# Attention in two layers: exponentials placed ahead of copies on ScalarE, and the rounding of output weights placed behind a head's step

## The chip, the cores and the metric

The kernel runs on one core of a Trainium2 chip. The metric is the device time of the whole program in microseconds. Five engines run side by side, each through an instruction list of its own in fixed order, and they wait for one another on semaphores: TensorE (PE, with PEld for its weight loads), VectorE (DVE), ScalarE (ACT), GpSimd (POOL) and SyncE (SP), whose queue loads the weights.

## The reference

Two transformer layers (an even and an odd one), then a block with a delta rule. Only the two attention mixers matter here. Each projects 256 tokens, runs 16 heads of width 64 over them, and multiplies the 16 heads' results by an output weight of 1024 x 1024:

```python
def even_mixer(xn, w_in, w_out, ...):
    qa, ka, va, qi, ki, wi, qb, kb, vb = _split(xn @ w_in, EVEN_SPLITS)
    ...
    ya = dsa_sparse_attention(qa, ka, va, qi, ki, wi)      # kind A: keys picked by top_k
    yb = chunked_relpos_attention(qb, kb, vb, rel_bias)    # kind B
    return jnp.concatenate([ya, yb], axis=-1) @ w_out

def odd_mixer(xn, w_in, w_out, forget_b, sinks, rope_h):
    qc, kc, vc, fc, qd, kd, vd = _split(xn @ w_in, ODD_SPLITS)
    ...
    yc = forgetting_attention(qc, kc, vc, log_f)           # kind C
    yd = sink_window_gqa(qd, kd, vd, sinks)                # kind D
    return jnp.concatenate([yc, yd], axis=-1) @ w_out

# every kind:  p = softmax(q @ k.T * scale + bias or mask);  y = p @ v
```

Everything is float32. A product with weights is done as three products of rounded halves: high x high, high x low, low x high.

## The kernel before

**Weights.** All weights come as a stream of slots of 128 x 2048 numbers. For each slot SP loads `raw` (ring of 3), ACT writes the rounded half `whi` (`split`, L1839, 128x2048), and the remainder `wlo = raw - whi` follows: on DVE (L2370, 128x2048), or, for the *shared* slots, its second half on DVE (L2366, 128x1024) and its first half on POOL (L1022, 128x1024). The slots of the last two output groups and the first slots of the next stage are shared ones. PE multiplies with L1182 to L1184. A slot is split two slots ahead of its use (AHEAD = 2), and its `raw` buffer is loaded anew when both remainders are written.

**Positions.** A mixer is a list of positions `at` that each engine walks through in the same order. First come the projection parts, four to a block (`("proj", block, i)`; even 28 positions, odd 20), then 16 output parts, four to a group g (`("out", g, sub)`), each 6 products of 512 columns. At each position an engine does its share of the part and then calls `attend(layer, step)`, with step = at - 15 (even) or at - 11 (odd).

**Heads.** Heads go in pairs. Head e has step e in the odd layer; in the even layer heads 0 to 7 have steps 0 to 7 and heads 8 to 15 steps 12 to 19. So a pair's *first head* (even e) has an odd `at` and its *second head* (odd e) an even `at`. At the first head's step PE makes the logits of both (L1355). Then, for a head of step s:

- DVE at step s: logits plus bias and their minimum, from PSUM (L2635); the second head's directly behind the first's if its step comes next
- ACT at step s: two exponentials with their sums (L1992; kind D also one of the sinks, L1990)
- scaling by 1/sum: for heads 0 to 7 on POOL (L1032, L1035), for heads 8 to 15 on DVE at step s+1 (L2641, L2644, two instructions of 128x128 and 128x256)
- PE at step s+2: three transposes into bank 6 (L1323); they wait for the scaling and for ACT's copy of the head before, since there is one bank
- ACT at step s+2: copy of bank 6 to `probT` (L1978)
- behind a pair's second head, at the position three behind its step: PE sums the values of the pair (L1336), ACT rounds them (`mhi`, L1982), DVE writes the remainder (`mlo`, L2649)

**ACT's order at a position before the change:** copy of a block (L1936), `split` of a slot, copy of turned tiles (L1944), then attend: `probT` of head s-2, `mhi`, exponentials of head s. In a projection part the split stands at i = 0 and 2, in the output at the first part of each group. **DVE's order:** `split` (in the output at the second part of each group), then attend: minimum of head s, scaling of head s-1, `mlo`. Three output splits have an effect: those at the first parts of groups 0, 1 and 2.

The lines of PE that show the transposes' two waits:

```python
pe.wait_ge(*S["probs_copied"].at((layer, e - 1)))
pe.wait_ge(*S["probs_scaled" if e < POOL_HEADS else "probs_divided"].at((layer, e)))
for j in range(3):
    last = nc.tensor.transpose(ps[:, 6, j * P:(j + 1) * P], prob[:, e % 3, j * P:(j + 1) * P], ident)
```

Of the kernel before, what the change touches and what calls it, by code (L numbers as in the profile page):

```python
# [46 lines left out]
AHEAD = RING - 1  # L47
# [77 lines left out]
OUT_SLOT = (2, 3, 0, 1)  # L125
# [350 lines left out]
def out_order(layer, g):  # L476

    return (0, 1, 2, 3) if g else FIRST_PARTS[layer]
# [4 lines left out]
FIRST_STEP = {"even": 4 * 3 + 3, "odd": 4 * 2 + 3}  # L483
# [13 lines left out]
def step_at(layer, s):  # L497

    return STEPS[layer][s] if 0 <= s < len(STEPS[layer]) else NOTHING


def head_at(layer, s):

    what, e = step_at(layer, s)
    return e if what == "head" else None
# [19 lines left out]
def mixed_tile(p):  # L525

    return 2 * OUT_SLOT[p // 2] + p % 2
# [93 lines left out]
def build(nc, dram, counted, stop=None):  # L621
# [3 lines left out]
    slot_of = {}  # L625
# [3 lines left out]
    with ctx:  # L629
# [1199 lines left out]
        def _(act):  # L1829
            split_to = [0]  # L1830

            def split(last):

                while split_to[0] <= min(last, len(plan) - 1):
                    n = split_to[0]
                    act.wait_ge(weights_loaded[n % RAW], 16 * (n // RAW + 1))
                    if n >= RING:
                        act.wait_ge(*S["weights_used"].at(n - RING))
                    act.activation(used(whi, n), used(raw, n), ACT.Copy).then_inc(*S["weights_high"].one((n, 1)))  # L1839
                    split_to[0] += 1  # L1840
# [130 lines left out]
            def attend(layer, s):  # L1971

                e = head_at(layer, s - 2)
                if e is not None:
                    act.wait_ge(*S["probs_turned"].at((layer, e)))
                    if e >= 4:
                        act.wait_ge(*S["values_done"].at((layer, (e - 4) // 2)))
                    act.activation(probT[:, e % 4, :], ps[:, 6, 0:3 * P], ACT.Copy).then_inc(*S["probs_copied"].one((layer, e)))  # L1978
                p = pair_at(layer, s - 3)
                if p is not None:  # L1980
                    act.wait_ge(*S["values_done"].at((layer, p)))
                    act.activation(mhi[:, mixed_tile(p), :], ps[:, 7, p % 2 * TOK:(p % 2 + 1) * TOK], ACT.Copy)\  # L1982
                        .then_inc(*S["mixed_high"].one((layer, p)))
                e = head_at(layer, s)
                if e is not None:
                    kind, h = head_of(layer, e)
                    for t in range(TT):
                        act.wait_ge(*S["logits"].at((layer, e, t)))
                        if t == TT - 1 and kind == "D":
                            act.activation(sunk[:, e % 4, :], lowest[:, e % 4, :], ACT.Exp, bias=row_at["sinks"][:, h:h + 1])  # L1990
                        at = prob[:, e % 3, tile_logits(t)]
                        last = act.activation(at, at, ACT.Exp, bias=lowest[:, e % 4, t:t + 1], scale=-1.0,  # L1992
                                              accum_out=total[:, e % 4, t:t + 1])
                    last.then_inc(*S["exps"].one((layer, e)))
# [252 lines left out]
            first_norm()  # L2247
            for li, (layer, blocks) in enumerate(LAYERS):
                for at, place in enumerate(POSITIONS[layer]):
                    if at == 4 * len(blocks) and blocks[-1][0] not in ROTATED:  # L2250
                        copy_block(layer, blocks, len(blocks) - 1, 1)
                    if place:
                        what, a, i = place
                        if what == "proj":
                            if i % 2 == 0:
                                split(slot_of[((layer, blocks[a][0]), i // 2)] + AHEAD)
                            if i == 3 and blocks[a][0] not in ROTATED:
                                copy_block(layer, blocks, a, 0)
                            if i == 0 and a and blocks[a - 1][0] not in ROTATED:
                                copy_block(layer, blocks, a - 1, 1)  # L2260
                        elif i == out_order(layer, a)[0]:
                            split(slot_of[(f"{layer}_out", OUT_SLOT[a])] + AHEAD - (a == 3))
                    if place in TURNS[layer]:
                        copy_turned(layer, blocks, *TURNS[layer][place])
                    if layer == "even" and place in INDEX_AT:
                        index_relus(INDEX_AT[place])
                    if layer == "odd" and place == ("proj", 1, 1):
                        gate_logs()
                    if layer == "odd" and place == FORGET_SPLIT_AT:
                        forget_high()  # L2270
                    attend(layer, at - FIRST_STEP[layer])
                norm_behind_out(2 * li + 1, slot_of[(f"{layer}_out", OUT_SLOT[3])])
                up(li)
                norm_behind_down(2 * li + 2, slot_of[(f"down{li}", FT // 2 - 1)])
# [75 lines left out]
        def _(dve):  # L2350
# [69 lines left out]
            def norm_behind_out(k, last):  # L2420

                add_to_x(k, last, 0, (0, 1), 0)
                split(last + 2)
                normalize(k, [0])
                add_to_x(k, last, 1, (0,), 0)
                lows(k, [(0, 0), (0, 1)])
                add_to_x(k, last, 1, (1,), 0)
                normalize(k, [1])
                lows(k, [(1, 0), (1, 1)])
# [537 lines left out]
            for li, (layer, blocks) in enumerate(LAYERS):  # L2967
                for at, place in enumerate(POSITIONS[layer]):
                    if layer == "even" and place == ("proj", 0, 3):
                        dve.wait_ge(consts_loaded, 16)  # L2970
                        dve.wait_ge(rows_loaded, 16)
                        dve.wait_ge(ident_loaded, 16)
                        dve.tensor_tensor(pick_row[:, 0:8], ident[:, 0:8], ident[:, 32:40], ALU.add)\
                            .then_inc(*S["rows_low"].one("pick"))
                    if place:
                        what, a, i = place
                        if what == "proj":
                            if i == 3 and blocks[a][0] in ROTATED:
                                rope_block(layer, blocks, a, 0)
                            if i == 0 and a and blocks[a - 1][0] in ROTATED:  # L2980
                                rope_block(layer, blocks, a - 1, 1)
                            if i % 2:
                                split(slot_of[((layer, blocks[a][0]), i // 2)] + AHEAD)
                        elif i == out_order(layer, a)[1]:
                            split(slot_of[(f"{layer}_out", OUT_SLOT[a])] + AHEAD - (a == 3))
                    if layer == "even":
                        if place == ("proj", 1, 2):
                            for t in range(TT):
                                index_keys(t)
                        if place == ("proj", 2, 2):  # L2990
                            dve.wait_ge(*S["bias_ready"].at(1))
                            link(dve.tensor_scalar(bias[:, :, :], bias[:, :, :], 8.0, None, ALU.mult))
                        if place in INDEX_AT:
                            index_sums(INDEX_AT[place])
                        if place in TOP_AT:
                            take_top(TOP_AT[place])
                        if place == ("proj", 6, 1):
                            pick()
                    else:
                        if place == ("proj", 1, 0):  # L3000
                            gate_inputs()
                        if place == ("proj", 1, 2):
                            gate_finish()
                            dve.wait_ge(*S["gate_made"].at("sinks"))
                        if place == FORGET_SPLIT_AT:
                            forget_low()
                        if place in FORGET_AT:
                            forget_biases(FORGET_AT[place])
                    attend(layer, at - FIRST_STEP[layer])
                norm_behind_out(2 * li + 1, slot_of[(f"{layer}_out", OUT_SLOT[3])])  # L3010
                up(li)
                norm_behind_down(2 * li + 2, slot_of[(f"down{li}", FT // 2 - 1)])
# [131 lines left out]
```

## Time and profile before

| | |
|---|---|
| median of 3 runs | 1208.64 us (1208.52 to 1208.86) |
| the profiled execution | 1204.78 us, of which the span of the trace is 1203.0 us |
| busy: PE, DVE, ACT, POOL | 97%, 70%, 58%, 27% of the span |
| mean granted clock of TensorE | 0.997 |
| loads of weights | 1024 KB each, 4.8 us from issue to landing |
| even mixer, output parts | from 102.5 to 135.9 us of the span |
| odd mixer, heads and output parts | from 350.9 to 418.5 us of the span |

The timeline of one engine, cut to a few microseconds, gives each instruction's start and duration; in square brackets stands how long the engine was idle before it, and what ended that. Rows of different engines are put side by side by their start times. The table's last two rows are the two stretches to which the change belongs.

### The profile page before, as it was taken

The numbers are of one execution on the slowest core, as the hardware profiler recorded it, in microseconds if no ns is written. First come the engines' busy times: TensorE is split into PE (matmuls) and PEld (weight loads), VectorE is DVE, ScalarE is ACT, GpSimd is POOL, SyncE is SP. The second block draws the span as 40 slices with busy tenths as digits, with TensorE's granted clock in tenths as the row PEclk, the third lists the DMA queues.
The fourth block names the chain that finished last, engine by engine and source line by source line (L and its number), as shares of the span: only waits on it lengthen the run. The fifth ranks groups of instructions, "written<-read, shape, count | busy, mean of one in ns | idle before, by whom it ended". The sixth has DMA issues, their size and how long they took to land.

```text
span 1203.0 us, 21393 instructions
## 1 busy us (share of the span) xinstructions
PE 1170.6 (97%) x8616; PEld 1087.1 (90%) x8616; DVE 841.6 (70%) x1519; ACT 701.7 (58%) x1181; POOL 320.0 (27%) x257
## 2 busy tenths in 40 slices
PE   8999999999999999999999999999999999999997
PEld 7777899998877799998889999998989989999886
DVE  6796588884675579885568787888954565555456
ACT  5475576663458566664366667766667445444344
POOL 1172200000016300000166666575555320000000
PEclk9999999999999999999999999999999999999999
DMA  7633355556553356555343332332222646555542
GB/s 285 252 140 140 123 211 206 184 181 219 175 191 125 129 208 219 196 208 210 128 160 126 121 115 105 133 114 98 94 83 106 227 170 224 210 183 203 202 155 81
DMA packets 31587, 199.74 MB, mean 166 GB/s; under 512 B 4289, under 2 KB 6481, under 8 KB 8706
## 3 DMA queue, kind: packets, MB, share of 16 engines
q1 hardware_dynamic: 29506, 189.27, 43.6%
q0 software_dynamic: 1840, 8.60, 1.9%
q8 instruction: 68, 1.11, 0.4%
q10 hardware_dynamic: 144, 0.52, 0.1%
q14 instruction: 29, 0.24, 0.1%
HBM read 197.33 MB, written 1.05 MB: 165 GB/s over the span
## 4 chain that ended last, share of the span: by engine, by line
PE 83%; DVE 8%; ACT 4%; issue 2%; POOL 1%; DMA 0%; SPq 0%; POOLq 0%; DVEq 0%; ACTq 0%
PE ps L1182 24%; PE ps L1183 23%; PE ps L1184 23%; PE ps L1559 1%; PE ps L1575 1%; DVE ps L2824 1%; DVE wlo L2370 1%; PE ps L1336 1%; DVE conv L2755 1%; PE ps L1355 1%; PE ps L1323 1%; PE ps L1189 1%; PE ps L1207 1%; DVE halves L2472 1%; PE ps L1276 1%
## 5 line engine op out<-in xcount | busy, mean ns | idle before, releaser
L1182 PE MATMUL ps<-halves,whi 128*128 128x256 f32 x1472 | 409.8, 278 | 0.2
L1184 PE MATMUL ps<-halves,wlo 128*128 128x256 f32 x1472 | 404.8, 275 | 0.0
L1183 PE MATMUL ps<-halves,whi 128*128 128x256 f32 x1472 | 404.8, 275 | 0.0
L2370 DVE TENSOR_TENSOR wlo<-raw,whi 128x2048 fp32r<-128x2048 f32 (+1 forms) x133 | 301.3, 2268 | 112.2 <-ACT whi L1839 108.7
L1839 ACT ACTIVATE whi<-raw 128x2048 fp32r<-128x2048 f32 (+1 forms) x143 | 269.5, 1887 | 102.4 <-PE ps L1184 96.3
L1182 PEld LDWEIGHTS ps<-halves,whi 128*128 128x128 f32 x1472 | 282.5, 192 | 0.8 <-DVE halves L2963 0.5
L1184 PEld LDWEIGHTS ps<-halves,wlo 128*128 128x128 f32 x1472 | 282.6, 192 | 0.0
L1183 PEld LDWEIGHTS ps<-halves,whi 128*128 128x128 f32 x1472 | 282.5, 192 | 0.1
L1106 POOL TENSOR_TENSOR wlo<-raw,whi 128x1024 fp32r<-128x1024 f32 x72 | 172.5, 2404 | 51.0 <-ACT whi L1848 50.4
L1000 POOL TENSOR_TENSOR rstd<-sumsq,half_power 128x1 f32<-128x1 f32 x14 | 11.3, 809 | 573.3 <-ACT xn L1866 406.0
L1182 PE MATMUL ps<-whi,halves 128*128 128x512 f32 (+4 forms) x440 | 148.2, 337 | 4.8 <-DVE halves L2472 4.0
L1184 PE MATMUL ps<-whi,halves 128*128 128x512 f32 (+4 forms) x440 | 143.8, 327 | 0.0
L1183 PE MATMUL ps<-wlo,halves 128*128 128x512 f32 (+4 forms) x440 | 143.7, 327 | 0.0
L1182 PE MATMUL ps<-whi,hhi 128*128 128x512 f32 x264 | 100.2, 379 | 0.5 <-DVE hf L2689 0.5
L1183 PE MATMUL ps<-wlo,hhi 128*128 128x512 f32 x264 | 100.1, 379 | 0.0
L1184 PE MATMUL ps<-whi,hlo 128*128 128x512 f32 x264 | 100.1, 379 | 0.0
L1182 PEld LDWEIGHTS ps<-whi,halves 128*128 128x128 f32 x440 | 83.6, 190 | 16.0 <-issue 8.5
L2824 DVE SCALAR_TENSOR_TENSOR ps<-glu_in,par,ps 128x256 f32<-128x256 f32 x224 | 94.5, 480 | 0.0
L1184 PEld LDWEIGHTS ps<-whi,halves 128*128 128x128 f32 x440 | 83.8, 190 | 5.8
L1183 PEld LDWEIGHTS ps<-wlo,halves 128*128 128x128 f32 x440 | 83.7, 190 | 4.9
L2017 ACT ACTIVATE cv<-ps,par 128x256 f32<-128x256 f32 x88 | 44.9, 561 | 73.3 <-PE ps L1184 67.2
L1848 ACT ACTIVATE whi<-raw 128x1024 fp32r<-128x1024 f32 x72 | 76.5, 1064 | 7.8 <-PE ps L1184 7.8
(337 smaller groups left out, 1849.5 us busy)
## 6 DMA issues: line engine op xcount, KB each, us to landing
raw<-in_stream SPq DMA_DIRECT2D x176, 1024.0 KB, 4.8
gain<-in_gains POOLq DMA_DIRECT2D x7, 512.0 KB, 5.7
bias<-in_rel POOLq DMA_DIRECT2D x1, 1536.0 KB, 8.6
raw<-in_stream SPq DMA_DIRECT2D x2, 648.0 KB, 7.3
cst<-in_consts POOLq DMA_DIRECT2D x1, 1280.5 KB, 5.9
raw<-in_stream SPq DMA_DIRECT2D x2, 528.0 KB, 4.2
x<-in_x SPq DMA_DIRECT2D x2, 512.0 KB, 4.3
out<-xn SPq DMA_DIRECT2D x4, 256.0 KB, 2.5
```

Source lines behind the costliest of these rows:

```text
L1106: pool.tensor_tensor(wlo[:, n % RING, c], raw[:, n % RAW, c], whi[:, n % RING, c].bitcast(F32), ALU.subtract).then_inc(*S["pool_weights_lo ...
L1182: nc.tensor.matmul(out, a_hi, b_hi, start=start, stop=False)
L1183: nc.tensor.matmul(out, a_hi, b_lo, start=False, stop=False)
L1184: return nc.tensor.matmul(out, a_lo, b_hi, start=False, stop=stop)
L1189: nc.tensor.matmul(ps[:, bank, 0:P], ident, ident, start=True, stop=True)
L1207: last = nc.tensor.transpose(to_evens_first(out) if k in TOKENS_EVENS_FIRST else out, xn[:, t, (4 * half + i) * P:(4 * half + i + 1) * P], ...
L1276: last = nc.tensor.transpose(ps[:, 3, i * P:(i + 1) * P], temp[:, b % 2, t, i * P:(i + 1) * P], ident)
L1839: act.activation(used(whi, n), used(raw, n), ACT.Copy).then_inc(*S["weights_high"].one((n, 1)))
L1848: act.activation(whi[:, n % RING, c], raw[:, n % RAW, c], ACT.Copy).then_inc(*S["weights_high"].one((n, half)))
L2017: act.activation(cv[:, j % 2, m, :], ps[:, up_bank(j), m * TOK:(m + 1) * TOK], ACT.Identity, bias=par_at(f"conv_b{li}", c), scale=par_at(f ...
L2370: dve.tensor_tensor(used(wlo, n), used(raw, n), used(whi, n).bitcast(F32), ALU.subtract)\
L2824: dve.scalar_tensor_tensor(odd_taps[:, :] if k == 29 else sums, src, w, sums, ALU.mult, ALU.add)\
```

## The change

No instruction is added or taken away; three things are moved.

- ACT, at even positions of the odd layer (from the projection on) and of the even layer's output parts: the exponentials of step s, which are those of a second head, come first at the position, ahead of the block copy, the split, the turned copy, `probT` and `mhi`. At odd positions they stay where they were.
- ACT: the splits of the output groups come behind attend and the exponentials of their position.
- DVE: the splits of the output groups come behind attend of their position.

```diff
@@ scalar: attend is cut in two
                     act.activation(mhi[:, mixed_tile(p), :], ...)
+
+            def exponentials(layer, s):
+
                 e = head_at(layer, s)
@@ scalar: the positions
                 for at, place in enumerate(POSITIONS[layer]):
+                    step = at - FIRST_STEP[layer]
+                    exps_ahead = at % 2 == 0 and (at >= 4 * len(blocks) or layer == "odd")
+                    if exps_ahead:
+                        exponentials(layer, step)
                     if at == 4 * len(blocks) and blocks[-1][0] not in ROTATED:
                         copy_block(layer, blocks, len(blocks) - 1, 1)
...
-                        elif i == out_order(layer, a)[0]:
-                            split(slot_of[(f"{layer}_out", OUT_SLOT[a])] + AHEAD - (a == 3))
...
-                    attend(layer, at - FIRST_STEP[layer])
+                    attend(layer, step)
+                    if not exps_ahead:
+                        exponentials(layer, step)
+                    if place and place[0] == "out" and place[2] == out_order(layer, place[1])[0]:
+                        split(slot_of[(f"{layer}_out", OUT_SLOT[place[1]])] + AHEAD - (place[1] == 3))
@@ vector: the positions
-                        elif i == out_order(layer, a)[1]:
-                            split(slot_of[(f"{layer}_out", OUT_SLOT[a])] + AHEAD - (a == 3))
...
                     attend(layer, at - FIRST_STEP[layer])
+                    if place and place[0] == "out" and place[2] == out_order(layer, place[1])[1]:
+                        split(slot_of[(f"{layer}_out", OUT_SLOT[place[1]])] + AHEAD - (place[1] == 3))
```

## Rows read from the trace of the kernel before

**Rows 1.** The page, part 1: busy us (share of the span) xinstructions.

```profile
PE 1170.6 (97%) x8616; PEld 1087.1 (90%) x8616; DVE 841.6 (70%) x1519; ACT 701.7 (58%) x1181; POOL 320.0 (27%) x257
```

**Rows 2.** PE's waits, whole span: waiter <- awaited: us, times, longest us.

```profile
PE ps L1323 <- DVE prob L2644: 2.1, 1, 2.1
...
PE ps L1323 <- ACT probT L1978: 1.5, 3, 0.9
```

**Rows 3.** Timeline of PE, even output parts: start, duration, what [idle before].

```profile
105.63 0.93 PE L1355 MATMUL ps<-fm 64*128 64x128 f32 x8
...
110.18 0.52 PE L1323 MATMUL ps<-ident,prob 128*128 128x128 f32 x3 [2.13 <-DVE prob L2644]
...
111.83 0.49 PE L1323 MATMUL ps<-ident,prob 128*128 128x128 f32 x3
...
113.05 0.93 PE L1355 MATMUL ps<-fm 64*128 64x128 f32 x8
...
117.56 0.55 PE L1323 MATMUL ps<-ident,prob 128*128 128x128 f32 x3 [0.28 <-ACT probT L1978]
...
121.24 0.52 PE L1323 MATMUL ps<-ident,prob 128*128 128x128 f32 x3
...
122.90 0.49 PE L1323 MATMUL ps<-ident,prob 128*128 128x128 f32 x3
```

**Rows 4.** Timeline of ACT, the same stretch.

```profile
104.33 1.90 ACT L1839 ACTIVATE whi<-raw 128x2048 fp32r<-128x2048 f32 x1
...
110.73 0.49 ACT L1978 ACTIVATE probT<-ps 128x384 f32<-128x384 f32 x1 [2.03 <-PE ps L1323]
...
114.34 0.40 ACT L1992 ACTIVATE prob<-prob,lowest 128x128 f32<-128x128 f32 x1 [0.79 <-DVE lowest L2635]
...
115.23 1.90 ACT L1839 ACTIVATE whi<-raw 128x2048 fp32r<-128x2048 f32 x1
117.03 0.47 ACT L1978 ACTIVATE probT<-ps 128x384 f32<-128x384 f32 x1
```

**Rows 5.** Timeline of DVE, the same stretch.

```profile
106.25 1.23 DVE L2366 TENSOR_TENSOR wlo<-raw,whi 128x1024 fp32r<-128x1024 f32 x1 [1.53 <-ACT whi L1839]
107.39 0.28 DVE L2635 CUSTOM_DVE_ANT_0 prob<-ps,picked 128x128 f32<-128x128 f32 x1
...
108.14 1.89 DVE L2644 TENSOR_SCALAR prob<-prob,inverse 128x128 f32<-128x128 f32 x2
109.95 0.28 DVE L2635 CUSTOM_DVE_ANT_0 prob<-ps,picked 128x128 f32<-128x128 f32 x1
...
114.01 0.29 DVE L2635 CUSTOM_DVE_ANT_0 prob<-ps,picked 128x128 f32<-128x128 f32 x1 [2.76 <-PE ps L1355]
...
115.23 0.41 DVE L2649 TENSOR_TENSOR mlo<-ps,mhi 128x256 fp32r<-128x256 f32 x1
115.57 0.28 DVE L2635 CUSTOM_DVE_ANT_0 prob<-ps,picked 128x128 f32<-128x128 f32 x1
```

**Rows 6.** Timeline of POOL, the same stretch.

```profile
106.30 3.39 POOL L1022 TENSOR_TENSOR wlo<-raw,whi 128x1024 fp32r<-128x1024 f32 x1 [15.25 <-ACT whi L1839]
...
132.98 2.38 POOL L1022 TENSOR_TENSOR wlo<-raw,whi 128x1024 fp32r<-128x1024 f32 x1 [3.07 <-ACT whi L1839]
```

**Rows 7.** Timeline of PE, odd layer.

```profile
359.26 0.52 PE L1323 MATMUL ps<-ident,prob 128*128 128x128 f32 x3 [1.63 <-POOL prob L1035]
...
389.08 0.55 PE L1323 MATMUL ps<-ident,prob 128*128 128x128 f32 x3 [0.94 <-ACT probT L1978]
...
394.42 0.49 PE L1323 MATMUL ps<-ident,prob 128*128 128x128 f32 x3
```

**Rows 8.** Timeline of DVE, odd layer, first heads.

```profile
356.04 2.29 DVE L2370 TENSOR_TENSOR wlo<-raw,whi 128x2048 fp32r<-128x2048 f32 x1 [1.98 <-ACT whi L1839]
```

**Rows 9.** Timeline of POOL, the same stretch.

```profile
356.38 2.74 POOL L1035 TENSOR_SCALAR prob<-prob,inverse 128x256 f32<-128x256 f32 x1
```

**Rows 10.** Timeline of ACT, odd layer, split at the first output part.

```profile
386.76 1.90 ACT L1839 ACTIVATE whi<-raw 128x2048 fp32r<-128x2048 f32 x1
```

## The prediction, made before the result was known

> **What bounds the kernel now.** First the page's busy shares: PE is busy for 97% of the span [rows 1]. So nothing that the other engines do counts unless PE waits for it, and all that a new order can give is PE's idle time. Then PE's list of waits, for the transposes of the scaled exponentials (L1323) alone: one wait of 2.1 us for DVE's scaling, three of 1.5 us together for ACT's `probT` [rows 2]; in PE's timeline of the odd layer one of 1.63 us for POOL's scaling [rows 7]. Together some 5 us, 0.4% of the time: the ceiling of the gain. Then the timelines of PE, ACT, DVE and POOL beside one another, in the output parts, to see what stood in front of what. There ACT's rounding (1.90 us) stands before `probT` at 117.03, and PE's transpose follows it at 117.56 [rows 3, 4]: the wait that the change aims at. The wait at 110.18 is another matter. DVE's two scaling instructions started at 108.14 and took 1.89 us [rows 5]; POOL's half of a split ran from 106.30 to 109.69, and the scaling ended 0.34 us behind it, at 110.03 [rows 5, 6].
>
> **Rules that I read from the rows.** (a) POOL's half takes 2.38 us undisturbed and 3.39 us when DVE's half (1.23 us) began 0.05 us before it [rows 5, 6]; so these two exclude each other, and so do POOL's half and DVE's scaling: whichever starts first finishes. The minimum (one operand in PSUM) at 107.39 was not held up by POOL's half [rows 5]. The Trainium skill (SBUF — State Buffer, Who interferes with whom) states that the read and write ports that VectorE shares with GpSimd are an exclusive lock, taken by a VectorE instruction with two SBUF inputs or in a two-port mode, and that issue order alone decides who blocks. That speaks against this change: by that rule the sum below is +4.8 us, and without it -0.3 us; the rows agree with the rule. (b) POOL's half starts 0.07 us behind ACT's rounding (104.33 + 1.90 = 106.23, POOL 106.30) [rows 4, 6]. (c) DVE's first minimum of a pair starts 0.96 us after PE's logits (113.05, 114.01), the second head's 1.56 us later (115.57), ACT's exponentials 0.33 us after the minimum, and they take 0.89 us (114.34 to 115.23) [rows 3 to 5]. (d) A minimum with the reciprocal takes 0.75 us (107.39 to 108.14), `mlo` 0.34 us (115.23 to 115.57), DVE's half 1.14 us until the next instruction (106.25 to 107.39) [rows 5]. (e) `probT` starts 0.55 us after its transpose (110.18, 110.73), the next transpose 0.53 us after `probT` starts (117.03, 117.56), and 0.15 us after the scaling (110.03, 110.18) [rows 3 to 5]. (f) An output part and a transpose take PE 1.65 us (110.18 to 111.83), the values between a transpose and the logits bring it to 1.22 us (111.83 to 113.05) [rows 3].
>
> **Even layer, group 0.** ACT: the exponentials of head 9 come before the last block copy, so the split starts at 104.33 + 0.90 = 105.23 and ends at 107.13; POOL's half starts at 107.20. DVE: its half no longer stands before the minimum of head 10, which starts at 105.63 + 0.96 = 106.59, and the scaling of head 9 is due at 107.34. That is 0.14 us too late: POOL has the ports until 107.20 + 2.38 = 109.58, the scaling ends at 109.92, and PE's transpose is at 110.07 instead of 110.18. The wait stays. Behind the scaling now stands DVE's half (next instruction 0.08 us before the scaling's end plus 1.14: 110.98), and only then the minimum of head 11, which stood at 109.95 before [rows 5]. ACT now takes the exponentials of head 11 *before* `probT` of head 9: they start at 110.98 + 0.33 = 111.31 and end at 112.20, `probT` follows, PE's transpose of head 10 is at 112.73, before it was at 111.83: **+0.9 us**.
>
> **Even layer, group 1.** Logits of heads 12 and 13 at 112.73 + 1.22 = 113.95. Minimum of head 13 at 113.95 + 0.96 + 1.56 = 116.47, its exponentials on ACT 116.80 to 117.69, then `probT` of head 11 and the transpose of head 12 at 118.22 (+0.66 against 117.56, so here 0.24 us come back: the wait that the change removes). The split starts 0.38 us after `probT`, at 118.07, ends at 119.97; POOL's half runs from 120.04 to 122.42. DVE: logits at 118.22 + 1.22 = 119.44, minimum of head 14 at 120.40, scaling of head 13 due at 121.15, in the middle of POOL's half. Before, POOL's half had started three microseconds earlier, 0.07 us behind the rounding of 115.23 to 117.13 [rows 4], and was over. The scaling ends at 122.42 + 0.34 = 122.76, the transpose of head 13 at 122.91 instead of 121.24 (+1.67). Then `mlo` (0.34) and DVE's half (1.14), so the minimum of head 15 at 122.68 + 1.48 = 124.16; its exponentials 124.49 to 125.38, `probT` of head 13 behind them, the transpose of head 14 at 125.91 instead of 122.90: +3.0 [rows 3]. In group 2 no minimum and no exponentials are left, and the split, now behind `probT`, gives back some 0.09 us (my estimate from PE's idle time there) before the last pair's values: 3.01 - 0.09 = **+2.92 us**.
>
> **Odd layer, projection.** For the first pair POOL's second scaling instruction took 2.74 us from 356.38, because DVE's remainders (2.29 us) had started at 356.04 [rows 8, 9]. The exponentials of head 1 now stand before ACT's split and push it and these remainders back by about 1.1 us, to 357.1. By then POOL is done at some 357.3 at the latest (0.9 us is my estimate for 128x256: 2.74 less the time until DVE's end at 358.33, plus start-up), and PE, which was ready at 359.26 - 1.63 = 357.63, doesn't wait: **-1.6 us** [rows 7]. The later D heads have nothing to gain, and need about 0.3 us of luck once (head 2's scaling must start before DVE's remainders).
>
> **Odd layer, output.** The split at 386.76 [rows 10] would stand at 385.13 by that gain; the exponentials of head 9 (0.89) and `probT` of head 7 (0.38) go before it: 386.40, to 388.30. `probT` starts at 386.02 and the transpose of head 8 is at 386.55, before it was at 389.08 - 1.63 = 387.45: -0.9, the wait of 0.94 is gone [rows 7]. Then the same trap: POOL's half 388.37 to 390.75, scaling of head 9 until 391.09, `mlo` and DVE's half until 391.01 + 1.48 = 392.49, exponentials of head 11 until 392.82 + 0.89 = 393.71, transpose of head 10 at 394.24 against 394.42: -0.2 is left of 2.5. Group 1 costs what it costs in the even layer, 3.01 - 0.90 = 2.11, less 0.09: -0.18 + 2.02 = **+1.84 us**.
>
> **Other queues.** SP's loads wait for the remainders of the slot three back. Those come 1.4 us later in group 0 (DVE's half ends at 111.07 instead of POOL's at 109.69) and some 3 us in group 1, and the next split into such a buffer stands more than a group later: no wait. POOL has nothing else to do between its halves. Cost of these, and of the splits being later for PE: nothing, since they run two slots ahead; without that cover each would cost up to a rounding and its remainders, some 4 us.
>
> **Sum.** 2.92 + 1.84 = +4.8 us: the profiled execution goes from 1204.78 to 1209.6 us. The median of the runs stood 3.9 us above it, 1208.64, and moves with it: **1213.4 us**. Bounds: each of the four output groups is good to some 0.3 us, and the 0.14 us by which POOL comes first in group 0 may fall the other way: then head 9 gains 2 us and head 10 stands where it stood (POOL's half then holds up the scaling of head 10), 1.0 us less. That gives +3.3 to +5.8, 1211.9 to 1214.4.
>
> **Rivals.** (1) *The halves do not shut each other out as I read it*, the long scaling at 108.14 being chance. Then the scalings of heads 9 and 13 are on time, but DVE's half still stands before the minimum of the second head, and that before `probT`. By the same steps without POOL's hold each layer stands at -1.2 behind group 0 (the odd one with its projection's gain counted in), and group 1 costs +1.1: -0.1 and -0.2 in the end, 1208.3. Against it: the rows of both engines fit to 0.1 us. (2) *The change does what it is for*: the exponentials' wait for their minimum costs nothing, and the waits of rows 2 and 7 go without a successor: -4 to -5 us, 1204. It needs DVE's halves to find room where I see none. (3) *Dearer still, on the side of the forecast*: in the odd projection DVE's remainders start before POOL's second scaling instruction for head 2 or another; the scaling then ends 2.3 us later and PE waits about 2 us more: 1215.4. (4) *A gain with the blocking*, that is, DVE's scaling is first in both groups of both layers: it decides from 0.14 us in group 0, but from 1.1 us in group 1, hence only a part of it is counted in the bounds.
>
> **Chances.** Forecast 0.70, rival 1 0.13, rival 2 0.08, rival 3 0.09. The range takes in the forecast's bounds, most of rivals 1 and 3: 1207.9 to 1215.6. About 0.2% (2.4 us) is what a measurement of this kernel can tell from no change. Faster by more than that: rival 2, 0.08. Within it: rival 1 and the forecast's lower edge, 0.15. Slower: 0.77.
>
> **What would show it.** Right: waits of PE L1323 for DVE L2644 near 2 us at the even layer's head 9 and over 1 us at the odd one's and at head 13 of both, and in each layer two instructions of L2644 of 1 to 2.5 us; new waits of 1 us or more for ACT `probT` at heads 10 and 14; ACT's L1992 waiting for DVE's minimum with `probT` behind it; no wait for POOL at the odd layer's first head. Wrong: scalings of 0.3 us beside a running POOL half, or a minimum of head 11 before DVE's half. What would overturn it: any stretch outside the two mixers that gets shorter, since I count nothing there.

## The result, and the profile after

| | before | after |
|---|---|---|
| median of 9 runs each | 1207.56 us (1204.21 to 1208.86) | 1210.87 us (1209.26 to 1212.97) |
| ratio after / before | | 1.0032, 95% interval 1.0023 to 1.0042 |
| profiled execution, its span | 1204.78, 1203.0 us | 1210.73, 1208.8 us |
| mean granted clock in it | 0.997 | 0.994 |

The change makes the kernel slower by 0.32%, or 3.9 us (2.8 to 5.1); forecast were +4.8 us. With six more runs, the median of before is 1207.56 us and no longer 1208.64: 1.1 us of the distance between 1213.4 us and the measured 1210.87 us come from that base. By its lower base the measured median also lies under the forecast's inner bounds of 1211.9 to 1214.4 us, while the difference, +3.9 us, lies inside its +3.3 to +5.8.

PE's waits for the transposes in the kernel after (waiter <- awaited: us, times, longest us), to be set beside [rows 2]:

```profile
PE ps L1323 <- DVE prob L2653: 4.9, 4, 2.0
PE ps L1323 <- ACT probT L1978: 4.3, 4, 1.2
PE ps L1323 <- POOL prob L1035: 0.2, 1, 0.2
```

Before there were 2.1 us in one wait for DVE's scaling and 1.5 us in three for `probT`; now there are four and four, 9.2 us together. Waits for POOL were 1.8 us in two and are 0.2 in one: the wait of 1.63 us at the odd layer's head 0 is gone, and the 0.2 us that is left stands at the even layer's head 0 (at 63.77, before at 64.26), which the change doesn't touch. (The exponentials are L1995 now, the minimum L2644, the scaling L2653, DVE's half L2375.)

PE's timeline of the kernel after, even output parts, beside [rows 3]. It runs 0.49 us ahead of that of before (logits of heads 8 and 9: 101.17 instead of 101.66):

```profile
101.17 0.93 PE L1355 MATMUL ps<-fm 64*128 64x128 f32 x8
...
109.53 0.52 PE L1323 MATMUL ps<-ident,prob 128*128 128x128 f32 x3 [1.97 <-DVE prob L2653]
112.17 0.55 PE L1323 MATMUL ps<-ident,prob 128*128 128x128 f32 x3 [0.83 <-ACT probT L1978]
113.45 0.93 PE L1355 MATMUL ps<-fm 64*128 64x128 f32 x8
...
117.70 0.55 PE L1323 MATMUL ps<-ident,prob 128*128 128x128 f32 x3
118.98 0.93 PE L1355 MATMUL ps<-fm 64*128 64x128 f32 x8
122.38 0.52 PE L1323 MATMUL ps<-ident,prob 128*128 128x128 f32 x3 [0.98 <-DVE prob L2653]
125.35 0.55 PE L1323 MATMUL ps<-ident,prob 128*128 128x128 f32 x3 [1.16 <-ACT probT L1978]
...
129.75 0.87 PE L1336 MATMUL ps<-probT,v 128*64 128x256 f32 x8
```

DVE's timeline beside it [rows 5], one instruction of each pair of minima:

```profile
106.09 0.29 DVE L2644 CUSTOM_DVE_ANT_0 prob<-ps,picked 128x128 f32<-128x128 f32 x1 [1.86 <-PE ps L1355]
106.65 0.16 DVE L2650 RECIPROCAL inverse<-total 128x2 f32<-128x2 f32 x1
106.85 2.53 DVE L2653 TENSOR_SCALAR prob<-prob,inverse 128x128 f32<-128x128 f32 x2
109.31 1.21 DVE L2375 TENSOR_TENSOR wlo<-raw,whi 128x1024 fp32r<-128x1024 f32 x1
110.44 0.28 DVE L2644 CUSTOM_DVE_ANT_0 prob<-ps,picked 128x128 f32<-128x128 f32 x1
...
120.69 1.54 DVE L2653 TENSOR_SCALAR prob<-prob,inverse 128x128 f32<-128x128 f32 x2
122.16 0.41 DVE L2658 TENSOR_TENSOR mlo<-ps,mhi 128x256 fp32r<-128x256 f32 x1
122.49 1.21 DVE L2375 TENSOR_TENSOR wlo<-raw,whi 128x1024 fp32r<-128x1024 f32 x1
123.62 0.28 DVE L2644 CUSTOM_DVE_ANT_0 prob<-ps,picked 128x128 f32<-128x128 f32 x1
```

POOL [rows 6] and ACT [rows 4] of the same stretch:

```profile
106.68 2.36 POOL L1022 TENSOR_TENSOR wlo<-raw,whi 128x1024 fp32r<-128x1024 f32 x1 [16.13 <-ACT whi L1839]
119.52 2.37 POOL L1022 TENSOR_TENSOR wlo<-raw,whi 128x1024 fp32r<-128x1024 f32 x1 [10.48 <-ACT whi L1839]
```

```profile
110.76 0.40 ACT L1995 ACTIVATE prob<-prob,lowest 128x128 f32<-128x128 f32 x1 [2.91 <-DVE lowest L2644]
...
111.65 0.47 ACT L1978 ACTIVATE probT<-ps 128x384 f32<-128x384 f32 x1
...
123.94 0.40 ACT L1995 ACTIVATE prob<-prob,lowest 128x128 f32<-128x128 f32 x1 [2.69 <-DVE lowest L2644]
...
124.83 0.47 ACT L1978 ACTIVATE probT<-ps 128x384 f32<-128x384 f32 x1
```

So one chain is read across four engines. POOL's half begins at 106.68, 0.17 us ahead of DVE's scaling (106.85), and ends at 109.04; the scaling, 0.55 us where nothing holds it, ends at 109.38. Then DVE's half, and only then head 11's minimum (110.44). ACT stood idle for 2.91 us waiting for it, *with `probT` of head 9 behind it in its queue* (111.65), and PE got its bank for head 10 at 112.17. The second group repeats this with the larger delay.

The mixers of the two traces, from the first logits to the last values:

| | before | after | difference | forecast |
|---|---|---|---|---|
| even (heads 8 and 9 on) | 101.66 to 127.24 | 101.17 to 129.75 | +3.00 | +2.92 |
| odd, all heads | 350.89 to 409.83 | 353.39 to 414.24 | +1.91 | +1.84 |

Sum +4.91. The spans differ by 5.8: 0.5 less ahead of the even mixer, and 1.4 more behind the odd one, where nothing was changed (the way from the last values to the first L1489, transposes in the block with the delta rule, took 214.8 us before, 216.3 after). What differs there is the clock, in the windows of 4 us from 604 on (length, busy us and instructions of PE, PEld, DVE, ACT, POOL, the granted clock, DMA share and GB/s). Before:

```profile
604.00:608.00 4.00, 4.00 (x22) 3.70 (x22) 2.83 (x4) 2.24 (x3) 2.76 (x4) 0.57 0.33 98
608.00:612.00 4.00, 3.52 (x32) 3.33 (x31) 1.29 (x2) 1.09 (x2) 0.00 (x0) 1.00 0.39 164
```

After, the same stretch some 4 to 5 us later:

```profile
608.00:612.00 4.00, 4.00 (x20) 4.00 (x21) 3.08 (x5) 2.65 (x3) 2.76 (x4) 0.50 0.25 55
612.00:616.00 4.00, 3.97 (x26) 3.78 (x25) 1.54 (x3) 1.19 (x2) 0.00 (x0) 0.71 0.49 207
616.00:620.00 4.00, 4.00 (x28) 4.00 (x28) 2.17 (x7) 2.19 (x2) 1.01 (x1) 0.72 0.02 4
```

Not all of the slower stretch reaches the mark: at L1489 itself PE waited 1.58 us for DVE before and 0.39 us after. The way from the last values to L1489 took 214.8 to 218.4 us in the thirteen profiles of this study, all of which have the same work in it; before's was one of the two shortest. So one profile's span says little on 2 us; the mixers' marks, and the ratio of many runs, say more.

### The profile page after: what moved, and what is told of

Same layout as the page of the kernel before. It is cut to its first block, busy times and chain, and to the rows that moved or that the text cites. A ratio compares the mean times of both kernels' runs of the same rounds, so it can differ in the third digit from the quotient of the medians.

```text
span 1208.8 us, 21393 instructions
## 1 busy us (share of the span) xinstructions
PE 1174.4 (97%) x8616; PEld 1090.1 (90%) x8616; DVE 847.1 (70%) x1519; ACT 701.8 (58%) x1181; POOL 318.1 (26%) x257
## 4 chain that ended last, share of the span: by engine, by line
PE 84%; DVE 9%; ACT 3%; issue 2%; POOL 1%; DMA 0%; SPq 0%; POOLq 0%; DVEq 0%; ACTq 0%
PE ps L1182 24%; PE ps L1184 23%; PE ps L1183 23%; PE ps L1559 1%; PE ps L1575 1%; DVE ps L2833 1%; PE ps L1355 1%; PE ps L1336 1%; DVE conv L2764 1%; PE ps L1323 1%; DVE wlo L2379 1%; PE ps L1189 1%; PE ps L1207 1%; PE ps L1276 1%; DVE halves L2481 0%
```

## The experiments

All kernels compute the whole result; only the order or the sharing of work is changed (e10 adds matmuls whose result nothing uses). L numbers are those of the kernel after, except that the scaling is L2642 in the rows of e5. "Mixers" are the marks of the table above, against those of before.

| kernel | expected, us | measured ratio (95%) | in us | mixers, even / odd | clock falls in them |
|---|---|---|---|---|---|
| after | +4.8 | 1.0032 (1.0023 to 1.0042) | +3.9 | +3.00 / +1.91 | 0 / 0 |
| e1_exps_only | +3.7 | 1.0051 (1.0038 to 1.0065) | +6.2 | +4.02 / +3.62 | 1 / 2 |
| e11_exps_only_again | as e1 | 1.0056 (1.0043 to 1.0069) | +6.8 | +2.65 / +3.62 | 0 / 2 |
| e10_spins_in_wait | +4.8 | 1.0063 (1.0050 to 1.0077) | +7.6 | +5.15 / +1.25 | 1 / 0 |
| e2_splits_only | +5.7 | 1.0046 (1.0033 to 1.0059) | +5.6 | +3.38 / +3.18 | 1 / 0 |
| e3_odd_projection | -1.6 | 0.9987 (0.9976 to 0.9997) | -1.6 | +1.68 / -1.68 | 1 / 0 |
| e9_after_third_part | +0.6 | 1.0000 (0.9991 to 1.0009) | 0.0 | +0.83 / -0.36 | 0 / 0 |
| e7_before_unshared | -0.3 | 0.9998 (0.9988 to 1.0008) | -0.2 | -0.27 / -0.05 | 0 / 0 |
| e6_after_unshared | +4.1 | 1.0068 (1.0052 to 1.0084) | +8.2 | +3.74 / +3.40 | 1 / 1 |
| e4_second_scaling_first | -6.4 | 0.9929 (0.9915 to 0.9942) | -8.6 | -3.19 / -4.04 | 0 / 0 |
| e5_same_shared | e4 + 0.5 to 1.0 | 0.9939 (0.9927 to 0.9952) | -7.4 | -2.62 / -3.87 | 0 / 0 |
| e8_no_scale_first | e4 + 0.5 to 1.0 | 0.9948 (0.9933 to 0.9964) | -6.3 | -2.48 / -3.33 | 0 / 0 |

**e1_exps_only.** The exponentials ahead, as in after; the splits where they were before. Against after:

```diff
+                        elif i == out_order(layer, a)[0]:
+                            split(slot_of[(f"{layer}_out", OUT_SLOT[a])] + AHEAD - (a == 3))
...
-                    if place and place[0] == "out" and place[2] == out_order(layer, place[1])[0]:
-                        split(slot_of[(f"{layer}_out", OUT_SLOT[place[1]])] + AHEAD - (place[1] == 3))
```

(the same on DVE, with [1]).

> Second heads' exponentials ahead as in the changed kernel, but the rounding of output slots on ScalarE and VectorE in its old place. My theory (order on VectorE and GpSimd's hold on the shared ports; either move alone is dear): even layer +2.5 us (transpose of head 10 0.75 later, head 14 a further 1.8), odd layer +1.2 us (the projection's 1.6 gained and lost again), in all +3.7 us against the kernel before. Rival A (the exponentials ahead of probT are the whole trouble): about the changed kernel's +4.9. Rival B (the moved splits are the whole trouble): a gain of 1.6 to 3 us.

Measured +6.2 us, 2.5 more than the order of the instructions explains. The order is as expected; PE's timeline shows where the rest is:

```profile
110.93 0.87 PE L1323 MATMUL ps<-ident,prob 128*128 128x128 f32 x3 [3.00 <-DVE prob L2653]
113.95 0.49 PE L1323 MATMUL ps<-ident,prob 128*128 128x128 f32 x3
```

From one to the other 3.02 us instead of 1.65 (rule f), while nothing was waited for. The windows of 1 us give the cause, a granted clock of 0.50, which is the lower of TensorE's two levels, 1.2 GHz:

```profile
111.00:112.00 1.00, 1.00 (x4) 0.93 (x5) 0.96 (x5) 0.98 (x5) 0.00 (x0) 0.50 0.35 115
112.00:113.00 1.00, 1.00 (x4) 0.80 (x3) 0.00 (x0) 0.38 (x2) 0.00 (x0) 0.50 1.04 352
```

The odd mixer has two more such falls, each behind a wait of 1.8 us for `probT`.

**e2_splits_only.** The other part alone.

```diff
-                    exps_ahead = at % 2 == 0 and (at >= 4 * len(blocks) or layer == "odd")
+                    exps_ahead = False
```

> The rounding of output slots behind a head's step on both engines as in the changed kernel, exponentials all in their old place. My theory: scaling of heads 9 and 13 is held by GpSimd's half, VectorE's half then stands before the minimum of heads 11 and 15 and the scaling of heads 10 and 14: even layer +2.5, odd layer +3.2 us (no projection gain), in all +5.7 us. Rival A (exponentials ahead are the trouble): -1.3 us, since probT no longer waits behind the rounding. Rival B: +4 to +6.

Measured +5.6 us. The rival, by which the move of the splits was a gain, falls. Its waits in the output parts are all for the scaling:

```profile
PE ps L1323 <- DVE prob L2653: 8.6, 7, 2.0
```

By the ratios each part alone costs more than both together (+6.2 and +5.6 against +3.9 us), but both profiles have falls of the clock in their mixers and after's has none. With the falls taken out, the mixers stand at +3.9 us (e1, see e11 and e10 below) and about +5.6 (e2) against +4.9. The figure for e2 is worked out from its rows: head 10's scaling ends at 112.36, so without the fall its transposes would start at 112.51 (rule e) and head 11's at 112.51 + 1.22 + 2.41 = 116.14, while they started at 117.07. The fall cost 0.9 us there, of the 6.56. The two losses do not add up to 9.5 us. In both kernels a minimum or a scaling on DVE is late; that the other part then only moves what was waiting anyway is how I read it, and no run shows it by itself.

**e3_odd_projection.** The exponentials ahead in the odd projection alone, the splits where they were before. Against e1:

```diff
-                    exps_ahead = at % 2 == 0 and (at >= 4 * len(blocks) or layer == "odd")
+                    exps_ahead = at % 2 == 0 and at < 4 * len(blocks) and layer == "odd"
```

> Exponentials ahead only in the odd layer's projection parts, everything in the output parts as before. Both theories: -1.6 us, the wait of the transpose of the odd layer's head 0 for GpSimd's scaling is gone and nothing else moves. If the time does not fall, a gain in the middle of the program is taken back later.

Measured -1.6 us (-2.9 to -0.4), the odd mixer 1.68 us shorter: this part of the change is a gain, as forecast. The even mixer, whose instructions stand *in the order of before*, was 1.68 us longer in this profile:

```profile
110.57 0.67 PE L1323 MATMUL ps<-ident,prob 128*128 128x128 f32 x3 [2.14 <-DVE prob L2653]
113.59 0.80 PE L1323 MATMUL ps<-ident,prob 128*128 128x128 f32 x3
```

```profile
111.00:112.00 1.00, 1.00 (x5) 0.82 (x4) 0.60 (x3) 0.73 (x3) 0.00 (x0) 0.50 0.78 164
112.00:113.00 1.00, 1.00 (x4) 0.82 (x3) 0.00 (x0) 0.63 (x4) 0.00 (x0) 0.50 0.93 393
```

Behind the same wait before ([rows 3]: 2.13 us) the clock stayed at 1.00 and the step took 1.65 us. So the fall is not part of an order of instructions: it comes in one execution and not in another of the same stretch. What the order sets, as far as the ten falls in these mixers show, is how many places there are for it: each stands behind a wait of 1.8 us or more. The Trainium skill (TensorE: Matmul & The Clock Gate, What's actually happening) states, for a kernel's start, that one kernel runs a different number of matmuls at the lower clock from run to run. These two profiles show such a difference in the middle of a kernel.

**e9_after_third_part.** After, with DVE's half at the third part of the group in place of the second, that is, behind the second head's minimum instead of in front of it. One index:

```diff
-                    if place and place[0] == "out" and place[2] == out_order(layer, place[1])[1]:
+                    if place and place[0] == "out" and place[2] == out_order(layer, place[1])[2]:
```

> The changed kernel with one edit: VectorE's half of the remainders at the third part of a group, behind the second head's minimum, instead of the second part, before it. My theory: the scalings of heads 9 and 13 stay held by GpSimd, but the exponentials ahead of probT no longer wait 1.1 us more: even layer +0.9, odd layer -0.3, in all +0.6 us against the kernel before, 4.2 us faster than the changed kernel. If the place of this half does not matter: as the changed kernel, +4 to +5 us.

Measured 0.0 us, 3.9 less than after. The scaling is held up as in after (2.53 us), but what follows it is now the minimum:

```profile
107.06 2.53 DVE L2653 TENSOR_SCALAR prob<-prob,inverse 128x128 f32<-128x128 f32 x2
109.51 0.28 DVE L2644 CUSTOM_DVE_ANT_0 prob<-ps,picked 128x128 f32<-128x128 f32 x1
...
110.72 1.22 DVE L2375 TENSOR_TENSOR wlo<-raw,whi 128x1024 fp32r<-128x1024 f32 x1
```

and of PE's waits in the two stretches only the four for the scaling are left, 4.9 us; those for `probT` are gone. The mixers are 4.4 us shorter than after's (+0.83 - 0.36 against +4.91), where 4.2 were forecast. This names the main term: DVE's half in front of the minimum, for which ACT waits with `probT` behind it.

**e7_before_unshared.** A control: before, with DVE alone writing the remainders of the two later slots.

```diff
-        OUT_SHARED = {layer: [(f"{layer}_out", OUT_SLOT[2]), (f"{layer}_out", OUT_SLOT[3]), (f"up{li}", 0)]
+        OUT_SHARED = {layer: [(f"up{li}", 0)]
```

> Control: the kernel before, with POOL taken off the two later output slots, whose remainders DVE alone then computes (2.28 us each, whole, at the same second part). By the rule that POOL's half and DVE's scaling exclude each other, the scaling that took 1.89 us behind POOL's half takes 0.55, but DVE's own work ahead of the second head's minimum grows from 1.2 to 2.3 us, so that the wait of 2.1 us in the even group 0 shrinks little: about 0.3 us faster than before (ratio 0.9998). Rival: sharing itself was the cost in before; then this is 1.5 to 2 us faster (ratio 0.9985).

Measured -0.2 us. In PE's waits 2.1 us for the scaling became 1.85. POOL's hold and DVE's own whole instruction (2.29 us) cost the same in before's order; the rival falls.

**e6_after_unshared.** The same edit on after.

> The changed kernel, but VectorE alone writes the remainders of the two later output slots (2.3 us at once). No scaling can be held by GpSimd: each L2653 pair takes 0.55 us. My theory: the longer remainders still stand before the minimum of the second head, whose exponentials stand before probT: waits of L1323 for probT of about 2 us at heads 10 and 14, +4.1 us against the kernel before. A rival (GpSimd's hold is the whole of the loss): -0.3 to -2 us.

Measured +8.2 us, twice the forecast. The waits are all for `probT`, as DVE's 2.28 us now stand in front of the second head's minimum:

```profile
PE ps L1323 <- ACT probT L1978: 8.6, 4, 2.2
...
124.78 0.90 PE L1323 MATMUL ps<-ident,prob 128*128 128x128 f32 x3 [2.23 <-ACT probT L1978]
```

The mixers are 7.1 us longer. Two falls of the clock are in them: from the row above to the next transpose (129.03) 4.25 us against 2.67 between the same two in e11 (125.59, 128.26), and in the odd layer 5.20 against 3.69, together 3.1 us. (The 3.69 is the same step in e6's own even group 0, 111.52 to 115.21, where the clock stayed up.) Without them +4.0 us, the forecast to 0.1 us. So the order was rightly priced and the clock was left out. Whether POOL's help is worth having in after's order has two answers: by the order alone it costs 0.9 us (+4.9 with it, +4.0 without), by the ratios it saves 4.3 (+3.9 against +8.2). The waits are not longer in sum (8.6 against 9.2 us), but four of them last 1.9 to 2.2 us where after has one of 2.0, and in the profile two falls stand behind these four. The rival, by which POOL's hold is the whole of the loss, falls.

**e10_spins_in_wait and e11_exps_only_again.** e1 with dummy matmuls in PE's 3.00 us of idle time, and e1 once more beside it.

```diff
                         pe.wait_ge(*S["probs_copied"].at((layer, e - 1)))
+                    if layer == "even" and e == 9:
+                        spin(20, 6)
```

> The exponentials-only kernel, with 20 dummy transposes of the identity (128x128) put on PE between its two waits for the transposes of even head 9, so that PE works through most of the 3.00 us in which it stood idle there. In the exponentials-only kernel the clock was 0.50 from 111 to 113 us right behind that idle time, and the work up to the next transposes took 3.02 us instead of 1.65. If the fall of the clock comes from PE's idle time, the clock stays at 1.00 there and those 3.02 us become 1.65: 1.4 us less (about 1213.2 us, ratio 1.0040). The idle time shown goes from 3.00 to about 0.6 us, which by itself changes nothing, since the transposes still start when the scaling is done. Rival: the clock follows something else (the time of the run, the other engines), and it falls at the same place with the spins in; then the time stays at +6.2 us of before. The odd mixer's two falls behind waits of 1.83 us are left in both.

> The exponentials-only kernel once more, on the chip of these runs, as the direct partner of the kernel with spins. Theory: ratio 1.005 again, a wait of 3.00 us ahead of even head 9's transposes, the clock at 0.50 for some 2.5 us behind it. Rival: the falls are a chance of one profiled run, and stand elsewhere in this one, or are missing.

Both theories missed. In e11, without spins, the wait of 3.00 us is there and *no* fall behind it; the two falls of the odd layer are there again. In e10 there is none behind the spins, but none was in its partner either, and a new one came behind a wait of 1.82 us in the even group 1 (its part took 3.89 instead of 2.41 us); the odd layer, whose instructions are e1's, had none. The spins were also too many: 20 of them ran for 4.63 us, so the transposes came 1.3 us late. The row of PE in e10 (each spin is recorded as two):

```profile
107.79 4.63 PE L1189 MATMUL ps<-ident 128*128 128x128 f32 x40
```

So this pair doesn't decide whether work in the wait keeps the clock up; that stays open. It does give the price of the order alone: e11's even mixer (+2.65) and e10's odd one (+1.25) had no falls, +3.9 us together against the +3.7 expected of e1; and e1's even mixer differs from e11's by 1.37 us, one fall. The +6.2 and +6.8 us of the ratios are thus in part the clock.

**e4_second_scaling_first.** A version built from the theory: the exponentials ahead in the odd projection alone (e3); ACT's output splits behind the step; the remainders of the two later slots by DVE alone, and of all output slots at the group's third part, behind the minimum; and at even steps DVE scales the second head ahead of the next first head's minimum.

```diff
+                if s % 2 == 0:
+                    scale(layer, s - 1)
...
+                if s % 2:
+                    scale(layer, s - 1)
```

> Exponentials ahead in the odd projection only; in the output parts ScalarE's rounding behind the head's step as in the changed kernel; VectorE scales a second head before the next first head's minimum, writes the remainders of the two later output slots alone (GpSimd has no half of them) and at the third part of a group, behind its head's step. My theory: no wait of L1323 above 0.3 us is left in either layer's output; even layer -2.9, odd layer -3.5 us, in all -6.4 us. Rival A: the same order on ScalarE as e2 in the output, so -1.3 there and -1.6 in the projection: -2.9 us. If VectorE's whole remainder of 2.3 us is too long for the gaps: -2 to -4.

Measured -8.6 us, 1199.2 us: faster than both kernels. Of PE's waits in this line one is left:

```profile
PE ps L1323 <- POOL prob L1035: 0.2, 1, 0.2
```

PE is idle nowhere in its two mixers. The windows that span them, of before and then of e4 (length, PE's busy us and instructions, granted clock, DMA share, GB/s):

```profile
101.66:127.24 25.58, 23.17 (x142) 1.00 0.33 121
350.89:409.83 58.94, 56.09 (x342) 1.00 0.34 126
```

```profile
101.75:124.14 22.39, 22.39 (x141) 1.00 0.33 116
347.80:402.70 54.90, 54.90 (x341) 1.00 0.35 126
```

That is -7.2 us, 0.8 more than forecast: the 5.3 us of idle time (84.52 less 79.26) and another 2.0 us of what the rows call busy time for the same work. From the logits to the next transposes it is 2.26 us in e4 (110.82 to 113.08) and 2.41 before (113.05 to 115.46), and a transpose behind a wait is recorded at 0.52 or 0.55 us, one without at 0.49. So at least a part of the 2.0 us are short waits that PE's row doesn't show; e8 below has them alone. Why the ratio gives 1.4 us more than the mixers was not measured by itself; a kernel that offers no long wait for the clock to fall behind would do it.

**e5_same_shared and e8_no_scale_first.** e4 with one part of it undone each: POOL's half given back, and the scaling at its old place behind the minimum.

> The kernel of the fourth experiment (e4), but GpSimd again writes one half of the remainders of the two later output slots. My theory: GpSimd's half (2.2 us of hold, starting when ScalarE's rounding ends) meets only the scaling of the even layer's head 10, which ends about 0.5 us late; a second head's scaling is before it. So 0.5 to 1.0 us slower than e4, some -7.5 us against the kernel before. If the hold on the shared ports were the main trouble of the changed kernel in any order: 3 us or more slower than e4.

> The kernel of the fourth experiment (e4) without the scaling of a second head put first; scaling in the old order behind the next head's minimum. My theory: the transposes of heads 9, 11 and 13 wait 0.15 us each for the scaling in both layers: 0.5 to 1.0 us slower than e4. If e4's gain came from scaling second heads first: 4 us or more slower than e4.

e5 loses 1.2 us against e4 by the ratios (0.7 us in the mixers); its timeline of DVE has the hold again:

```profile
108.64 1.32 DVE L2642 TENSOR_SCALAR prob<-prob,inverse 128x128 f32<-128x128 f32 x2
109.89 1.21 DVE L2375 TENSOR_TENSOR wlo<-raw,whi 128x1024 fp32r<-128x1024 f32 x1
```

where e4 has 0.55 us. PE waits 0.38 us for it. The rival, by which POOL's hold is the main trouble in any order, falls.

e8 loses 2.3 us by the ratios, 1.4 us in the mixers (0.5 to 1.0 expected): the order of scaling and minimum is worth more than I gave it, and less than the 4 us of the rival. Its profile shows no wait for the scaling, and PE busy throughout both mixers as in e4. The wait is there all the same, DVE's row and then PE's:

```profile
112.94 0.55 DVE L2653 TENSOR_SCALAR prob<-prob,inverse 128x128 f32<-128x128 f32 x2
113.64 0.52 PE L1323 MATMUL ps<-ident,prob 128*128 128x128 f32 x3
```

The scaling ends at 113.49 and the transposes start 0.15 us behind it, the distance of rule (e), and 2.41 us after the logits of the next pair (111.23). In e4 the scaling of the same head ended at 112.08, a full 1.00 us ahead of its transposes, and these came 2.26 us after the logits. So a wait of 0.15 us stands in PE's busy time: the matmul in front of it (113.27, 0.38 us) is recorded until the transposes start. The intervals of e4, e5 and e8 overlap; it is the marks in the traces that order them.

## Why the prediction was right

**Rule (a), the halves and the scaling exclude each other: confirmed.** In after two pairs of scaling instructions (L2653) took 2.53 and 1.54 us in the even layer and two took 1.55 and 1.54 us in the odd one, each ending 0.3 us behind a POOL half's end; in e6 and e4, without POOL's half, the same pairs took 0.55. The Trainium skill's lock of the shared ports (SBUF — State Buffer, Who interferes with whom) agrees with these rows. Rival 1 (no exclusion) is out.

**Even layer, group 0.** Forecast transposes of heads 9 and 10 at 110.07 and 112.73; with the offset of 0.49 added they came at 110.02 and 112.66. POOL won the race by 0.17 us where I had said 0.14. The race that might have fallen the other way did not, in after and in e9.

**Even layer, group 1.** Forecast 118.22, 122.91, 125.91; with the offset 118.19, 122.87, 125.84. The wait the change aims at (0.28 at head 12) is gone from the list, though not wholly: PE's step there takes 1.84 us (115.86 to 117.70) against 1.65, and `probT` had started at 117.18, so some 0.2 us of it is left, as the forecast's 0.24 us given back had it. And the two that take its place are the 0.98 and 1.16 of the timeline.

**The estimate of 0.09 us given back in group 2 failed.** The last values are 3.00 us late, not 2.92: the sum without it would have been exact in the even layer, and +2.02 - 0.18 + 0.09 = +1.93 in the odd (measured +1.91). It is the one term that I took from no step.

**Odd projection.** -1.6 us forecast, -1.68 measured (e3). POOL's two scaling instructions of the first pair took 1.52 us instead of 3.33, as DVE's remainders came 1.1 us later (after: 359.60, behind POOL's start at 358.29). Rival 3, in which the remainders come first for another head, did not happen: PE waits nowhere for POOL in after's odd layer. Before, then after:

```profile
355.79 3.33 POOL L1035 TENSOR_SCALAR prob<-prob,inverse 128x128 f32<-128x128 f32 x2
```

```profile
358.29 1.52 POOL L1035 TENSOR_SCALAR prob<-prob,inverse 128x128 f32<-128x128 f32 x2
...
359.60 2.29 DVE L2379 TENSOR_TENSOR wlo<-raw,whi 128x2048 fp32r<-128x2048 f32 x1 [3.04 <-ACT whi L1839]
```

**Odd output.** Both groups as forecast: waits of 0.99 and 1.16, then 0.98 and 1.16 us, and the last values +1.91 (with the projection's gain in it) against +1.84.

**The signs.** All stand where they were forecast, four of them a little smaller than said: PE's waits of "over 1 us" for the scaling are 0.98 and 0.99 us, and the wait "of 1 us or more" at the even layer's head 10 is 0.83; the other three for `probT` are 1.16.

**Rival 2, the change does what it is for,** is out, but not for want of a gain: e4 took -8.6 us. I had called 5 us the ceiling, from PE's waits in [rows 2, 7]. As PE's idle time that was right (5.3 us). As a ceiling it was too low, and "all that a new order can give is PE's idle time" is the sentence that fails: e4 also took 2.0 us of recorded busy time, in part waits of 0.15 us that the matmul records cover (e8).

**The size.** Mixers +4.9 us against +4.8 forecast; ratio +3.9 us (2.8 to 5.1), which holds the forecast. The 1 us between them is less than the 3.6 us by which the stretch behind the mixers differs from profile to profile; what it consists of was not measured. What I did not count is this: a wait of PE also opens a place for a fall of the clock. After has no more such waits over 1.8 us than before (one each), and no fall in either mixer, so nothing was missed here; e1 and e6, with four each, show what it would have cost.

## What to carry over

When an instruction that waits is moved ahead of one that is ready, ask what the engine *it waits for* has queued in front of the answer: here ACT's exponentials stood idle for 2.9 us behind a 1.2 us subtraction on DVE that a POOL instruction had in turn delayed, and the ready `probT` behind them stopped PE. Move long work that nobody awaits behind the short work that somebody does, on every engine of the chain, before any one queue is reordered: one index on DVE took back 3.9 us, and the whole order 8.6 us. Where PE is 97% busy, a wait near 2 us can cost more than its length, and a short one can hide in the busy time; compare marks inside the trace, not spans.

## What the runs showed of the hardware

The clock's falls were the surprise. In the output parts of ten profiles (before, after, and e1, e2, e3, e6, e7, e9, e10, e11) PE had 21 waits of 1.8 us or more; behind ten of them the granted clock went from 1.00 to 0.50, for two or three whole windows of 1 us, at a cost of 0.9 (e2, where a part fell into a wait) to 1.7 us each. Behind a wait of 3.00 us it fell in e1 and not in e11, the same kernel; behind one of 2.1 us in e3 and not in before, the same order. Behind shorter waits, 1.64 us and less, I saw none in these stretches. Nor does length alone decide: 3.00 us once passed without a fall and 1.82 us more than once did not. The same happens outside the change, at 604 to 620 us, where the windows shown above have 0.57 for 4 us before and 0.50 to 0.72 for 12 us after, and there a shorter wait stood ahead of it: in the 40 us before the fall PE's only one was of 1.20 us (up to 601.55 before, 605.95 after). So 1.8 us is not a bound. What decides it in one execution these runs do not show.
